# Layer two's first expert tile picked and turned on chip instead of read back from memory

## The chip, the cores and the metric

The kernel runs on one core of a Trainium2 chip. The metric is the device time of one launch in microseconds. The median of three runs is given where two kernels are compared; traces come from one profiled execution each.

## The reference, cut to what matters

Two layers over 520 tokens (512 of a prompt, 8 samples) of width 1024. Each layer is a token mixer, a normalisation, and a mixture of 16 experts with top 2 routing. The part around the change is the second layer's expert stage:

```python
x = layer_norm(ALPHA * x + mix, ln1_g, ln1_b)        # the normed rows, X in the kernel
combine = route(t, w_router, router_bias)            # (tokens, 16), two weights a token
h = jax.nn.silu(jnp.einsum('td,edf->tef', t, w_gate)) * jnp.einsum('td,edf->tef', t, w_up)
y = jnp.einsum('tef,efd->td', h * combine[:, :, None], w_down)
x = layer_norm(ALPHA * x + y, ln2_g, ln2_b)
```

The gate and up products are 1024 to 512, the down product 512 to 1024, all in float32.

## The kernel before, in words

**Tokens in tiles.** X holds the 520 rows as five tiles of 128 partitions (`NT` = 5; the last has 8 rows), 1024 columns each.

**Slots.** The router gives each token two experts. VectorE works out a slot for each of them: expert e has the slots 96 e to 96 e + 95 (`CAP` = 96), and what is over goes to tiles behind. `r_slot[token, 16 i + e]` holds slot + 1 if token tile i's row goes to expert e, else 0. `choose`, `count` and `place_rows` do this; `place_rows` ends with two index lists, after which `shares` (weights), `tables` (which expert each tile takes, how many tiles; semaphore `tab_set`) and eight diagonal matrices follow on VectorE.

**Scatter and rows back.** GpSimd writes every row of X to its two slots in the DRAM buffer `expert_rows`: ten indirect transfers (`scatter`, semaphore `scat`). ScalarE waits for all ten (`scat` at 320), then issues `load_rows` for tile 0 and tile 1 (four transfers each), and scales the five tiles of X by ALPHA in place. VectorE turns the loaded rows in 32x32 blocks (`turn_rows`), which gives `xeT`, the tile with the width on the partitions.

**A tile on TensorE.** An expert tile is 64 products for each of gate, up and down (two records each, 128 records a block), with the output of the tile before turned back behind the first quarter of gate (eight transposes). ScalarE applies silu to gate (`sg_set`); VectorE turns the *next* tile's rows once that is done, and then multiplies by up (`h_set`), which down waits for. Tiles run in pairs in a loop; this input fills 16 tiles in a layer.

**Weights.** Two sets of buffers, 2 MB each for gate, up and down. SyncE's queue loads the set of tile t + 2 as tile t frees each buffer: gate when tile t's gate product is done (`gate_ps`), up after its up product, down after its down product. The weights of experts 0 and 1 of layer two are loaded earlier, during the mixer.

**Fillers.** Between the counts and the loop of layer two TensorE runs `keep_clock(24, 2, 512)`: products of constants, whose results nobody reads.

**End.** After the loop the results are gathered from DRAM, weighed on TensorE and normed.

Of the kernel before, what the change touches and what calls it, by code (L numbers as in the profile page):

```python
# [20 lines left out]
PAGE, NPAGES, NPHYS = 128, 8, 80  # L21
PAST = PAGE * NPAGES
BATCHES = DB // 2
LATE = P + 64
E, GROUPS, EPG, F = 16, 4, 4, 512
KF = F // P
CTX = 15
# [21 lines left out]
def rows_of(i):  # L49
    return P if i < NT - 1 else DB  # L50


def constants():

    parts, place, at = [], {}, 0

    def put(name, a, *dims):
        nonlocal at
        full = np.zeros((P, int(np.prod(a.shape[1:]))), np.float32)
        full[:a.shape[0]] = a.reshape(a.shape[0], -1)  # L60
        parts.append(full)
        place[name] = (at, dims or a.shape[1:])
        at += full.shape[1]

    def rowwise(v):
        return np.broadcast_to(np.asarray(v, np.float32).reshape(1, -1), (P, np.size(v)))

    i = np.arange(P)
    put("ident", np.eye(P))
    put("ones", np.ones((P, P)))  # L70
    put("before", (i[:, None] < i[None, :]))

    half = ROPE // 2
    inv = (np.float32(10000.0) ** (np.float32(-2.0) * np.arange(half, dtype=np.float32) / np.float32(ROPE)))
    pos = np.concatenate([np.arange(SEQ), np.full(DB, PAST)]).astype(np.float32)
    ang = pos[:, None] * inv[None, :].astype(np.float32)
    cos, sin = np.cos(ang).astype(np.float32), np.sin(ang).astype(np.float32)
    rot = np.concatenate([cos.T, cos.T, -sin.T, sin.T])
    one = np.ones((NOPE, TOK))
    put("rope_q", -SCALE * np.stack([np.concatenate([one, rot]), np.concatenate([rot, one])], 1))  # L80
    def natural(t):
        out = np.zeros((P, NT, half), np.float32)
        for j in range(NT):
            out[:rows_of(j), j] = t[P * j:P * j + rows_of(j)]
        return out
    put("cos_k", natural(cos))
    put("sin_k", natural(sin))

    put("causal", np.concatenate([np.zeros((P, SEQ - P)), np.where(i[None, :] > i[:, None], BIG, 0.0)], 1))
    own = np.full((P, BATCHES, DB), BIG)  # L90
    for u in range(BATCHES):
        for ab in range(2):
            own[32 * ab:32 * ab + 32, u, 2 * u + ab] = 0.0
    put("own_sample", own)

    band = np.zeros((P, 2, 4, BAND), np.float32)
    band_s = np.zeros((DB * CTX, 4, DB), np.float32)
    own_s = np.zeros((DB, 4, DB), np.float32)
    for g, w in enumerate(WINDOWS):
        for c in range(BAND):  # L100
            for r in range(max(0, c - w + 1), min(P, c + 1)):
                band[r, 0, g, c] = 1.0 / min(c + 1, w)
                band[r, 1, g, c] = 1.0 / w
            if c < P:
                band[c, :, g, c] -= 1.0
        for b in range(DB):
            band_s[b * CTX + CTX - w + 1:(b + 1) * CTX, g, b] = 1.0 / w
            own_s[b, g, b] = 1.0 / w - 1.0
    put("band", band)
    put("band_s", band_s)  # L110
    put("own_s", own_s)

    e = np.arange(E)
    put("slot0", rowwise(e * CAP))
    put("slot_over", rowwise((E - 1) * CAP - e * CAP))
    put("steps", rowwise(CAP * np.arange(1, KOV + 1)))
    put("before_e", rowwise(e[None, :] < e[:, None]), E, E)
    j = np.arange(EPG)
    put("earlier", rowwise(j[None, :] < j[:, None]), EPG, EPG)
    put("prefer", rowwise(GROUPS - np.arange(GROUPS)))  # L120
    put("real_row", (i < DB).astype(np.float32)[:, None])
    put("no_row", (i >= DB).astype(np.float32)[:, None])
    put("over_k", rowwise(np.arange(NOV)))
    put("even_k", rowwise(np.arange(0, NOV, 2)))
    put("expert", rowwise(e))
    put("reserve", rowwise(np.where(e < DENSE, 0, DB)))
    put("routed", rowwise(e >= DENSE))
    put("dense_row", np.where(e[None, :] < DENSE, TILES * CAP + DB * e[None, :] + np.minimum(i, DB - 1)[:, None], 0))
    put("ln_eps", np.full((P, 1), LN_EPS))
    put("rms_eps", np.full((P, 1), RMS_EPS))  # L130

    put("fold4", (i[:, None] % 32 == i[None, :] % 32))
    put("fold2", (i[:, None] % 64 == np.arange(64)[None, :]))
    return np.concatenate(parts, 1).astype(np.float32), place


def build(nc, t, consts_shape, place):

    ctx = ExitStack()
    with ctx:  # L140
# [119 lines left out]
        yl = [(ya[i], yb[i]) for i in range(3)] + [(view(arena, at, D), view(arena, at + D, D)) for at in (2048, 0)]  # L260
        diag = view(arena, 13104, NT - 1, 2, P)
        sum_at = (0, 2, 6, 4)
        mid_diag = view(C, place["rope_q"][0] + 512, 2, 2, P)
        alpha_id = view(C, place["causal"][0], P)

# [6 lines left out]
        def rt(n, *dims):  # L272
# [87 lines left out]
            sem(n) for n in ("lg_zero", "lg_ps", "lg_exp", "sel_set", "cnt_ps", "idx_set", "tab_set",  # L360
                             "scat", "xscaled"))
        dense, dense_st = sem("dense"), sem("dense_st")
        gath = [sem(f"gath{s}") for s in range(3)]
        diag_set, sum_ps, last_gath3, last_gath4 = (sem(n) for n in ("diag_set", "sum_ps", "last_gath3", "last_gath4"))
        last_gath, last_rows = gath + [last_gath3, last_gath4], (96, 96, 64, 32, 32)
# [51 lines left out]
        def _(sp):  # L417
# [55 lines left out]
            sp.wait_ge(pv_ps, 1)  # L473
            load_pages(sp, 0, 0, page_ld[0])
            load_pages(sp, 0, 1, page_ld[0])
            sp.dma_start(view(arena, 14656, LATE), t["consts"][:, held:]).then_inc(fold_ld, 16)
            load_pages(sp, 1, 0, page_ld[1])
            load_pages(sp, 1, 1, page_ld[1])
            sp.wait_ge(zero_st, 16 * (PAIRS - 1))
# [20 lines left out]
            for L in range(2):  # L500
# [20 lines left out]
                else:  # L521
                    sp.wait_ge(S[0]["xeT_set"], 2 * nh + 1)
                    sp.wait_ge(S[0]["xe_ld"][1], 64 * (nh + 1))
                    sp.dma_start(pscale, bcast(t["pool_scale"][0])).then_inc(st_ld, 16)
                    sp.dma_start(state[0:DB * CTX, :], t["state_pool"][0].rearrange("b c d -> (b c) d")).then_inc(st_ld, 16)

                    for slot, rows in ((0, 64), (1, 64), (2, 32)):
# [34 lines left out]
        def _(pe):  # L562
# [344 lines left out]
            def pool(i):  # L907

                pe.wait_ge(ln_out[0], NT + i + 1)
                if i < 4:  # L910
                    for g in range(2):
                        b = turn()
                        for c in range(4):
                            k = 4 * g + c
                            out = bank(b, 4, P)[:, c, :]
                            for at in (0, 64):
                                last = nc.tensor.matmul(out[at:at + 64, :], X[:, i, P * k + at:P * k + at + 64],
                                                        band[:, min(i, 1), k // 2, 0:P], start=True, stop=(i == 0))
                            for at in (0, 64) if i else ():
                                last = nc.tensor.matmul(out[at:at + 64, 0:CTX], X[:, i - 1, P * k + at:P * k + at + 64],  # L920
                                                        band[:, 1, k // 2, P:BAND], start=False, stop=True)
                        last.then_inc(turn_ps, 1)
                else:
                    b = turn()
                    pe.wait_ge(st_ld, 32)
                    for k in range(KD):
                        out = bank(b, KD, DB)[:, k, :]
                        for at in (0, 64):
                            nc.tensor.matmul(out[at:at + 64, :], state[0:DB * CTX, P * k + at:P * k + at + 64],
                                             band_s[0:DB * CTX, k // 2, :], start=True, stop=False)  # L930
                        for at in (0, 64):
                            last = nc.tensor.matmul(out[at:at + 64, :], X[0:DB, 4, P * k + at:P * k + at + 64],
                                                    own_s[0:DB, k // 2, :], start=False, stop=True)
                    last.then_inc(turn_ps, 1)
# [186 lines left out]
                router(1, i)  # L1121
            keep_clock(9, 2, 256)
            counts(3, 0, NT)
            keep_clock(24, 2, 512)
            experts(1)
            pe.wait_ge(xscaled, 2 * NT)
            pe.wait_ge(diag_set, 2)
# [112 lines left out]
        def _(act):  # L1240
# [103 lines left out]
            def experts(L):  # L1344
# [13 lines left out]
                    act.sem_inc(q["y_st"][s], 16)  # L1358

                if L:  # L1360
                    act.wait_ge(scat, 320)
                    load_rows(act, L, 0, slice(0, CAP))
                    load_rows(act, L, 1, slice(CAP, 2 * CAP))
                    for i in range(NT):
                        scale_rows(i)
# [112 lines left out]
        def _(dve):  # L1478
# [400 lines left out]
            def tables(L):  # L1879
# [16 lines left out]
                link(v.tensor_reduce(r_nov[one, :], r_nh[one, 0:NOV // 2], AXX, ALU.add))  # L1896
                v.tensor_scalar(n_half[one, :], r_nov[one, :], float(E // 2), None, ALU.add).then_inc(tab_set, 1)

            def experts(L):
                q = S[L]  # L1900
                dve.wait_ge(tab_set, 2 * L + 2)
# [6 lines left out]
                                xe[s].rearrange("p a (i m) -> p a m i", i=32).bitcast(mybir.dt.uint32)  # L1908
                                ).then_inc(q["xeT_set"], 1)

                dve.wait_ge(q["xe_ld"][0], 64)
                turn_rows(0, CAP if L else WIDE)
                if L == 0:
                    choose(0, 2, NT - 1, NT)

                def rows_back(tl, s, count):
                    dve.wait_ge(q["back_ps"], tl + 2)
# [59 lines left out]
            v.memset(bank(6, NT * E), 0.0).then_inc(lg_zero, 1)  # L1977

            dve.wait_ge(wp_ld, 16)
            dve.wait_ge(st_ld, 32)  # L1980
            v.tensor_scalar(alpha_id, ident, ALPHA, None, ALU.mult)
            wp4 = wpool.rearrange("p (g k) d -> p g k d", g=4)
            v.tensor_tensor(wp4, wp4, pscale.rearrange("p (g d) -> p g d", g=4).unsqueeze(2).to_broadcast([P, 4, 2, 256]),
# [10 lines left out]
            choose(1, 3, 0, NT)  # L1994
            count(1, 3, 0, NT)
            place_rows(1, 3, 0, NT)
            shares(1)
            tables(1)
            dve.wait_ge(mix_ps, 2 * NT)
# [60 lines left out]
```

## Time and profile before

| what | value |
|---|---|
| median of 3 runs | 1109.82 us (1109.48 to 1110.19) |
| the profiled execution | 1110.86 us |
| its span | 1109.2 us |
| TensorE busy | 1039.2 us (94%) |
| VectorE busy | 377.2 us (34%) |
| ScalarE busy | 195.8 us (18%) |
| GpSimd busy | 94.9 us (9%) |
| mean granted TensorE clock | 0.975 |
| moved by DMA | 297.24 MB, mean 268 GB/s |

The span runs from the first to the last instruction; the profiled time also holds what lies around it. The granted clock is TensorE's share of full speed. PE is TensorE, DVE is VectorE, ACT is ScalarE, POOL is GpSimd, SP is SyncE; a q behind a name is that engine's queue of transfers. A line number L is a line of the kernel. "x" counts instructions; a float32 product shows as two records, a transpose as one.

### The profile page before, as it was taken

Reading aid. Unit: us, or ns where it says so; the run is one execution under the profiler, and the core shown is the slowest. Engines: PE = TensorE matmul, PEld = TensorE weight load, DVE = VectorE, ACT = ScalarE, POOL = GpSimd, SP = SyncE. Lnnn points to the kernel's source line nnn. Section 1 sums busy time; section 2 is a strip of 40 time slices with the busy share of each in tenths; the row PEclk is TensorE's granted clock in tenths of the full one; section 3 lists DMA queues with packets and bytes.
Section 4 is the critical chain, followed back from the end, with each engine's and each line's share of the span. In section 5 each row is a group of like instructions: output and inputs, shape, how many; then the busy total and the mean of one; then the engine's idle time right before and its main releaser. Section 6 shows DMA issues by size and latency. Waiting matters only on the chain.

```text
span 1109.2 us, 36492 instructions
## 1 busy us (share of the span) xinstructions
PE 1039.2 (94%) x16051; PEld 878.1 (79%) x16051; DVE 377.2 (34%) x858; ACT 195.8 (18%) x444; POOL 94.9 (9%) x179
## 2 busy tenths in 40 slices
PE   7989999989999798999999999998899999999995
PEld 6767777744566398999999997675699999999982
DVE  1334444423366532121221212976112212212127
ACT  1234444430043121000000001111200000100010
POOL 0011121241000200000000002101100000000012
PEclk9999999989999889999999999988899999999999
DMA  9512342714205899999999997861599999999935
GB/s 337 196 56 90 121 145 90 256 35 135 88 14 215 333 360 331 361 374 397 375 383 374 388 389 240 312 276 66 188 368 399 385 394 371 379 393 384 401 102 218
DMA packets 80479, 297.24 MB, mean 268 GB/s; under 512 B 10216, under 2 KB 40304, under 8 KB 72095
## 3 DMA queue, kind: packets, MB, share of 16 engines
q1 hardware_dynamic: 54327, 248.91, 60.6%
q10 hardware_dynamic: 17952, 25.24, 6.8%
q0 software_dynamic: 8144, 22.29, 5.7%
q8 instruction: 41, 0.67, 0.2%
q14 instruction: 15, 0.12, 0.0%
HBM read 255.91 MB, written 40.97 MB: 268 GB/s over the span
## 4 chain that ended last, share of the span: by engine, by line
PE 81%; DVE 8%; DMA 4%; issue 3%; POOL 2%; ACT 1%; SPq 0%; ACTq 0%; POOLq 0%; DVEq 0%
PE PS L1000 16%; PE PS L1023 16%; PE PS L1012 15%; PE PS L895 5%; PE PS L648 4%; PE PS L695 3%; PE PS L985 3%; PE PS L711 3%; PE PS L603 2%; PE PS L704 2%; PE PS L625 2%; POOL expert_rows L1178 1%; PE PS L668 1%; PE PS L798 1%; PE PS L685 1%
## 5 line engine op out<-in xcount | busy, mean ns | idle before, releaser
L1000 PE MATMUL PS<-arena,ring 128*64 128x96 f32 (+1 forms) x4096 | 186.7, 250 | 8.0 <-DVE arena L1907 8.0
L1000 PEld LDWEIGHTS PS<-arena,ring 128*64 128x64 f32 x4096 | 177.0, 139 | 14.7 <-issue 14.7
L1023 PE MATMUL PS<-arena,ring 128*64 128x96 f32 (+1 forms) x4096 | 178.3, 248 | 10.1 <-DVE arena L1943 5.4
L1023 PEld LDWEIGHTS PS<-arena,ring 128*64 128x64 f32 x4096 | 173.8, 138 | 12.0 <-DVE arena L1943 6.5
L1012 PE MATMUL PS<-arena,ring 128*64 128x96 f32 (+1 forms) x4096 | 175.8, 246 | 0.7 <-issue 0.6
L1012 PEld LDWEIGHTS PS<-arena,ring 128*64 128x64 f32 x4096 | 171.9, 137 | 1.1 <-issue 1.1
L1907 DVE STREAM_TRANSPOSE arena<-arena 128x768 uint32<-128x768 uint32 x34 | 54.3, 1597 | 138.2 <-ACT arena L1384 124.0
L1951 DVE COPY arena<-PS 128x384 f32<-128x384 f32 x32 | 17.8, 557 | 160.9 <-PE PS L1023 160.9
L1395 ACT ACTIVATE arena<-PS 128x384 f32<-128x384 f32 x32 | 15.7, 490 | 252.8 <-PE PS L1023 252.8
L895 PE MATMUL PS<-ring,arena 128*128 128x512 f32 x128 | 57.2, 607 | 0.7 <-issue 0.7
L576 PE MATMUL PS<-C 128*128 128x256 f32 (+1 forms) x160 | 52.2, 483 | 0.2 <-issue 0.2
L895 PEld LDWEIGHTS PS<-ring,arena 128*128 128x128 f32 x128 | 24.7, 195 | 31.2 <-issue 31.2
L576 PEld LDWEIGHTS PS<-C 128*128 128x128 f32 x160 | 31.0, 196 | 20.0 <-issue 17.5
L648 PE MATMUL PS<-arena,ring 128*128 128x260 f32 x192 | 44.9, 384 | 1.2 <-POOL ring L1146 0.8
L695 PE MATMUL PS<-ring 128*128 128x512 f32 (+3 forms) x128 | 40.7, 463 | 1.8 <-ACT ring L1279 1.2
L1371 ACT ACTIVATE arena<-PS 96x512 f32<-96x512 f32 x32 | 18.9, 592 | 127.8 <-PE PS L985 119.6
L1919 DVE COPY arena<-PS 96x512 f32<-96x512 f32 x32 | 22.0, 687 | 56.7 <-PE PS L985 56.7
L648 PEld LDWEIGHTS PS<-arena,ring 128*128 128x128 f32 x192 | 35.2, 190 | 6.1 <-POOL ring L1146 1.0
L1157 POOL DMA_DIRECT2D ring<-cache_krope x64 | 34.5, 539 | 58.4 <-issue 58.4
L1287 ACT ACTIVATE ring<-PS,small 128x512 f32<-128x512 f32 (+1 forms) x64 | 33.0, 526 | 28.4 <-DVE small L1563 28.4
L695 PEld LDWEIGHTS PS<-ring 128*128 128x128 f32 x128 | 24.0, 198 | 17.1 <-issue 11.2
L1940 DVE TENSOR_TENSOR arena<-arena,PS 128x288 f32<-128x288 f32 (+1 forms) x32 | 14.6, 456 | 66.6 <-PE PS L1012 66.6
(300 smaller groups left out, 1113.1 us busy)
## 6 DMA issues: line engine op xcount, KB each, us to landing
ring<-w_up SPq DMA_DIRECT2D x32, 2048.0 KB, 18.1
ring<-w_down SPq DMA_DIRECT2D x32, 2048.0 KB, 20.9
ring<-w_gate SPq DMA_DIRECT2D x32, 2048.0 KB, 17.7
expert_out<-arena ACTq DMA_DIRECT2D x32, 384.0 KB, 13.9
arena<-expert_rows ACTq DMA_DIRECT2D x128, 96.0 KB, 9.5
expert_rows<-ring SPq DMA_DIRECT2D x6, 1920.0 KB, 9.9
ring<-cache_ckv SPq DMA_DIRECT2D x56, 128.0 KB, 2.2
expert_out<-ring SPq DMA_DIRECT2D x1, 4608.0 KB, 25.3
```

The lines of the kernel that those rows point to most:

```text
L576: nc.tensor.matmul(bank(b, cols), ident, idle_rows[:, 0:cols], start=True, stop=True)
L648: last = nc.tensor.matmul(bank(b, HALF), wuq[:, m, P * parity:P * (parity + 1)], cq[:, m, HALF * hf:HALF * (hf + 1)], start=(m == 0), stop ...
L695: nc.tensor.matmul(score(i), qT[par][:, P * i:P * (i + 1)], kT[par][:, 0:P * (i + 1)], start=True, stop=True).then_inc(s_ps, 1)
L711: last = nc.tensor.matmul(bank(3, 4, VH, off=256 * par)[at:at + 64, i, :], probT[:, i % 2, P * k + at:P * k + at + 64], V[odd][:, k, VH * ...
L895: last = nc.tensor.matmul(bank(b0 + hf)[0:n, :], oT[:, k, P * i:P * i + n], wo[:, k, 512 * hf:512 * (hf + 1)], start=(k == 0), stop=(k == ...
L985: last = nc.tensor.transpose(bank(4 + m // 4, 4, P)[0:CAP, m % 4, :], yT[:, m, :], ident)
L1000: last = nc.tensor.matmul(bank(s, KF, n)[at:at + 64, f, :], wg[w][:, k, P * f + at:P * f + at + 64], x[:, k, :], start=(k == 0), stop=(k = ...
L1012: last = nc.tensor.matmul(out[at:at + 64, :], wu[w][:, k, P * f + at:P * f + at + 64], x[:, k, :], start=(k == 0), stop=(k == KD - 1))
L1023: last = nc.tensor.matmul(bank(4 + m // 4, 4, n)[at:at + 64, m % 4, :], wd[w][:, f, P * m + at:P * m + at + 64], hh[:, f, :], start=(f == ...
L1157: pool_e.dma_start(krp[:, bass.ds(half, 1), ROPE * n:ROPE * (n + 1)], t["cache_krope"][0, bass.ds(page, 1), :, :].rearrange("a p d -> p a ...
L1287: nc.scalar.activation(prob[:, i, 0:P * (i + 1)], score(i), ACT.Exp, scale=-1.0, bias=mneg[:, c:c + 1], accum_out=rsum[:, c:c + 1]).then_i ...
L1907: v.transpose(xeT[n][s][:, :, 0:CAP].rearrange("p m (a j) -> p a m j", j=32).bitcast(mybir.dt.uint32), xe[s].rearrange("p a (i m) -> p a m ...
```

## The change

Tile 0 of layer two's loop no longer comes from `expert_rows`. After the slots are known, VectorE makes five 0/1 matrices `picked` (token rows x 96 slots: 1 where the row's slot for expert 0 is that column's). TensorE multiplies them with X, 512 columns at a time, over the five token tiles: this gives the 96 rows of tile 0 in two PSUM banks. ScalarE copies the halves to SBUF (`first_rows`), TensorE turns them by eight transposes (each of every eighth column), VectorE copies these into `xeT`. ScalarE only increments the semaphore of tile 0's rows in place of four loads. The filler products shrink. The slot numbers are 96 new columns of the constants, loaded by SyncE ahead of the pooling state; the scatters stay as they are, since tile 1 and later still read their rows back.

```diff
-LATE = P + 64
+LATE = P + 64 + 96
...
+    put("slot_no", rowwise(1 + np.arange(CAP)))
...
+        slot_no = view(C, place["causal"][0] + P, CAP)
+        first_rows = view(arena, 5120, D)
+        picked = view(C, place["rope_q"][0], NT, CAP)
...
+        picked_set, first_ps = sem("picked_set"), sem("first_ps")
...
                     sp.dma_start(pscale, bcast(t["pool_scale"][0])).then_inc(st_ld, 16)
+                    sp.dma_start(slot_no, t["consts"][:, held:held + CAP]).then_inc(st_ld, 16)
...
             counts(3, 0, NT)
-            keep_clock(24, 2, 512)
+            keep_clock(12, 2, 256)
+            pe.wait_ge(picked_set, 1)
+            for hf in range(2):
+                for i in range(NT):
+                    n = rows_of(i)
+                    last = nc.tensor.matmul(bank(hf)[0:CAP, :], picked[0:n, i, :], X[0:n, i, 512 * hf:512 * (hf + 1)],
+                                            start=(i == 0), stop=(i == NT - 1))
+                last.then_inc(first_ps, 1)
+            pe.wait_ge(picked_set, 3)
+            for k in range(KD):
+                last = nc.tensor.transpose(bank(2 + k // 4, 4, CAP)[:, k % 4, :],
+                                           first_rows[0:CAP, :].rearrange("b (p k) -> b k p", k=KD)[:, k, :], ident[0:CAP, 0:CAP])
+                if k % 4 == 3:
+                    last.then_inc(first_ps, 1)
             experts(1)
...
                 if L:
+                    for hf in range(2):
+                        act.wait_ge(first_ps, hf + 1)
+                        nc.scalar.activation(first_rows[0:CAP, 512 * hf:512 * (hf + 1)], bank(hf)[0:CAP, :], ACT.Copy
+                                             ).then_inc(picked_set, 1)
                     act.wait_ge(scat, 320)
-                    load_rows(act, L, 0, slice(0, CAP))
+                    act.sem_inc(q["xe_ld"][0], 64)
                     load_rows(act, L, 1, slice(CAP, 2 * CAP))
...
+            def pick_rows():
+
+                for i in range(NT):
+                    n = rows_of(i)
+                    ins = v.tensor_scalar(picked[0:n, i, :], slot_no[0:n, :], r_slot[0:n, E * i:E * i + 1], None, ALU.is_equal)
+                ins.then_inc(picked_set, 1)
...
-                dve.wait_ge(q["xe_ld"][0], 64)
-                turn_rows(0, CAP if L else WIDE)
                 if L == 0:
+                    dve.wait_ge(q["xe_ld"][0], 64)
+                    turn_rows(0, WIDE)
                     choose(0, 2, NT - 1, NT)
+                else:
+                    for c in range(2):
+                        dve.wait_ge(first_ps, 3 + c)
+                        ins = v.tensor_copy(xeT[CAP][0][:, 4 * c:4 * c + 4, :], bank(2 + c, 4, CAP))
+                    ins.then_inc(q["xeT_set"], 1)
...
             place_rows(1, 3, 0, NT)
+            pick_rows()
             shares(1)
             tables(1)
```

## Rows read from the trace of the kernel before

**Rows 1.** Windows: stretch; busy us PE, PEld, DVE, ACT, POOL; clock, DMA share, GB/s.

```profile
790.30:791.00 0.70, 0.63 (x8) 0.64 (x10) 0.00 (x0) 0.70 (x2) 0.00 (x0) 0.50 0.00 0
799.00:816.00 17.00, 17.00 (x397) 16.70 (x394) 3.55 (x5) 1.57 (x4) 0.00 (x0) 1.00 0.94 318
799.00:1064.00 265.00, 261.45 (x6011) 256.07 (x6008) 55.63 (x78) 23.88 (x46) 0.00 (x0) 1.00 1.00 377
943.50:960.50 17.00, 17.00 (x398) 16.70 (x396) 3.56 (x5) 1.57 (x3) 0.00 (x0) 1.00 1.02 379
977.50:995.50 18.00, 17.25 (x399) 16.80 (x397) 3.56 (x5) 1.57 (x3) 0.00 (x0) 1.00 1.03 394
```

**Rows 2.** Timeline of the SyncE queue, layer two's loop: start us, us, what.

```profile
798.96 0.35 SPq L488 DMA_DIRECT2D ring<-w_gate  x1
...
1033.40 0.40 SPq L496 DMA_DIRECT2D ring<-w_down  x1
```

**Rows 3.** DMA issues from 798 and from 1021: KB, us to landing.

```profile
ring<-w_down SPq DMA_DIRECT2D x1, 2048.0 KB, 13.6
...
ring<-w_down SPq DMA_DIRECT2D x1, 2048.0 KB, 30.2
```

**Rows 4.** Chain of waits, router of layer two to tile 0: start us, us, what.

```profile
768.48 0.25 DVE arena L1870
...
782.03 2.83 DMA expert_rows<-X,ids
...
788.66 1.58 DVE arena L1907
...
790.37 2.83 PE PS L1000 x32
793.20 1.45 PE PS L985 x8
...
804.04 5.28 PE PS L1023 x128
```

**Rows 5.** Timeline of GpSimd, the scatters.

```profile
769.90 1.01 POOL L1178 DMA_INDIRECT expert_rows<-X,ids  x1 [46.86 <-DVE ids L1877]
...
775.07 1.71 POOL L1178 DMA_INDIRECT expert_rows<-X,ids  x1 [0.30 <-issue]
...
782.03 0.85 POOL L1178 DMA_INDIRECT expert_rows<-X,ids  x1 [0.30 <-issue]
```

**Rows 6.** Timeline of TensorE, the fillers before layer two's loop.

```profile
764.17 20.80 PE L576 MATMUL PS<-C 128*128 128x512 f32 x48
```

**Rows 7.** Timeline of TensorE, the end of layer one's loop.

```profile
679.52 1.08 PE L985 MATMUL PS<-C,arena 128*96 128x128 f32 x8 [0.65 <-DVE arena L1951]
680.43 3.66 PE L1080 MATMUL PS<-X,C 128*128 128x512 f32 x8
```

**Rows 8.** Timeline of VectorE, diagonals and tile 0.

```profile
775.01 0.26 DVE L2001 TENSOR_SCALAR arena<-C,small 128x128 f32<-128x128 f32 x1
...
776.38 0.27 DVE L2002 TENSOR_SCALAR arena<-C,small 128x128 f32<-128x128 f32 x1
...
802.83 0.45 DVE L1940 TENSOR_TENSOR arena<-arena,PS 128x288 f32<-128x288 f32 x1 [1.91 <-PE PS L1012]
...
809.36 0.56 DVE L1951 COPY arena<-PS 128x384 f32<-128x384 f32 x1 [5.03 <-PE PS L1023]
```

**Rows 9.** Timeline of ScalarE and its queue, tile 0.

```profile
784.88 3.72 ACTq L406 DMA_DIRECT2D arena<-expert_rows  x8
788.65 2.00 ACT L1420 ACTIVATE X<-X 128x1024 f32<-128x1024 f32 x2 [30.21 <-issue]
...
793.51 1.28 ACT L1384 ACT_TABLE_LOAD   x1
798.80 0.49 ACT L1384 ACTIVATE arena<-PS 128x384 f32<-128x384 f32 x1 [4.01 <-PE PS L1000]
...
811.68 0.59 ACT L1371 ACTIVATE arena<-PS 96x512 f32<-96x512 f32 x1 [3.81 <-PE PS L985]
```

More of the change, by code:

```diff
@@ L475, in _ @@
             load_pages(sp, 0, 1, page_ld[0])
-            sp.dma_start(view(arena, 14656, LATE), t["consts"][:, held:]).then_inc(fold_ld, 16)
+            sp.dma_start(view(arena, 14656, P + 64), t["consts"][:, held + CAP:]).then_inc(fold_ld, 16)
             load_pages(sp, 1, 0, page_ld[1])
@@ L924, in pool @@
                     b = turn()
-                    pe.wait_ge(st_ld, 32)
+                    pe.wait_ge(st_ld, 48)
                     for k in range(KD):
@@ L1979, in _ @@
             dve.wait_ge(wp_ld, 16)
-            dve.wait_ge(st_ld, 32)
+            dve.wait_ge(st_ld, 48)
             v.tensor_scalar(alpha_id, ident, ALPHA, None, ALU.mult)
```

## The prediction, made before the changed kernel was timed

> **What bounds the kernel now.** I read the views in this order: busy time by stretch, the chain of waits between layer two's router and its first expert tile, each engine's timeline there, and the weight loads' issue and landing.
>
> By stretch, two things bound the expert loop one after the other [rows 1]. A tile takes 17.00 us while TensorE never rests, and from about 977 us on 18 us with 0.7 us of rest, because weights come late. Over the whole loop (799 to 1064 us) the DMA engines' share is 1.00. The last down weights are issued at 1033.40 and land 30.2 us later, at 1063.6, when the first tile's landed in 13.6 us [rows 2, 3]. So the backlog grows through the loop, and the last tile waits for a stream that has run without a break since 798.96, where the first tile's gate product freed its buffer. What moves that start, and keeps the stream fed, moves the end.
>
> Before the loop the chain goes: slots known on VectorE (768.48 + 0.25 = 768.73), ten scatters on GpSimd (769.90 to 782.03), their landing (784.86), the rows read back, a 32x32 turn (788.66, 1.58 us), tile 0 on TensorE at 790.37 [rows 4, 5]. The reader is to see that nothing before 784.9 is TensorE's: it runs dummy products [rows 6]. And the pause after them dropped its clock: the granted clock is 0.50, so 1.2 of 2.4 GHz, when tile 0 starts [rows 1], its first 32 records take 2.83 us where a quarter of a 128-record block's 5.28 is 1.32, and eight transposes 1.45 where they take 1.08 elsewhere [rows 4, 7]. Tile 0 pays about 1.9 us for that.
>
> **The change, part by part.**
>
> *Picks (VectorE).* Five compares of 128x96 after the slots. The nearest row is the 128x128 multiply by a column: eight from 775.01 to 776.65, 0.20 us apart [rows 8]. Each costs at most that, and at least the 0.1 that 96 of 128 columns leave of half of it; I take 0.17, so 0.85 us in all (0.5 to 1.0), and the picks are ready near 770.5. Queued behind them are shares, tables and the diagonals: the tables end 0.85 later, near 776, and who waits for those (ScalarE, TensorE, SyncE, GpSimd) needs them only after 776.
>
> *The picks beside GpSimd.* One scatter took 1.71 us instead of 0.85 to 1.01: the one that ran beside the eight multiplies [rows 5, 8]. That is 0.76 us for eight of them, so 0.5 us for five; bounds 0 and 0.85 (all of it). The scatters then land near 785.35. The Trainium skill (SBUF — State Buffer, "Who interferes with whom") says that a tensor_scalar in a two-port mode shuts GpSimd out for its whole length; by that rule the cost is the full 0.85 and an estimate of the end 0.35 us later than in the sum below. The trace leans the same way, with a smaller number.
>
> *Row products (TensorE).* The fillers shrink from 24x512 to 12x256 columns. 48 records of 512 columns took 20.80 us, 0.433 each [rows 6]; 24 of half the width take 5.2, from 764.17 to 769.4. Then 1.1 us of rest for the picks, and 2x5 products of 512 columns, two records each: 20 x 0.433 = 8.7 us, 770.5 to 779.3. The eight-row tile costs as much as the others.
>
> *Copies, transposes, copies.* ScalarE copies each half, 96x512, 0.59 us [rows 9]; it is idle. The second ends near 780.0. Eight transposes: 1.08 us [rows 7], though mine read every eighth column; bounds 1.08 and 1.45. VectorE copies two 128x384 pieces, 0.56 each by the same shape [rows 8]; the first lies beside the second four transposes, so 780.0 + 1.1 + 0.7 with the steps between. Tile 0's input is ready at **781.9** instead of 790.24. TensorE reads the loop count just before; after the first layer's loop it did so behind eight transposes without a gap [rows 7], so I take nothing, bound 2 us.
>
> *Tile 0, first half.* TensorE never rests over 1.2 us, so I take full clock: gate 5.28 + 1.08 = 6.4 us, free at **788.3** instead of 798.96, which is 10.6 us earlier: 8.4 from the start, the rest from the clock. Up ends at 793.6 instead of 804.04.
>
> *Tile 0, second half: a new wait.* Its down product needs the gate's activation, and what stands ahead of that in ScalarE's queue moves by far less than tile 0 does. It waits for the scatters (785.35), issues four row loads instead of eight (3.72 us for eight, so 1.9: 787.2), scales five tiles of X (788.65 to 793.51, so 4.86: 792.1), loads a table (1.28: 793.4), activates (0.49: 793.9) [rows 9]. VectorE then turns tile 1's rows ahead of the multiply: 1.6 us, 795.5, and multiplies, 0.45 [rows 4, 8]: 796.0. Before, this queue was done at 794.8, ahead of the gate product at 798.8, and nobody waited for it; now TensorE waits 2.4 us. Down takes 5.28 and ends at **801.3** instead of 809.3 [rows 4]: **8.0 us earlier**. All tiles after run 8.0 earlier while TensorE bounds.
>
> *The cover this gives.* Even if TensorE's part costs 2 us more than I say (slow clock, slow transposes, a late loop), up still ends before 796, and tile 0's end doesn't move. The row loads of tile 1 land by about 788, before use.
>
> *The stream.* Gate and up loads start 10.6 and 10.5 us earlier, the down load 8.0. 2.4 us more lie between the up and down issues, in which the engines may run dry. In the stretch after 798.96 they moved 318 GB/s at a share of 0.94 [rows 1], 3.3 MB of the 4.2 of gate and up by the time down was issued, so at the loop's mean of 377 some 2.4 us of work was left, and little of the gap is idle. The stream's end thus moves by 8.0 (no lead kept) to 10.6 us (all kept). I take 9.0, between the two and nearer the lower, since part of the gap may still run empty. The four row loads less (96 KB each) lie before the stream and don't count. The new load of the slot numbers (48 KB) stands in SyncE's queue at the end of layer one's loop, where TensorE next runs fillers until the gathered rows land, so I take nothing, at most the 0.35 us of one issue [rows 2].
>
> **Sum.** 1110.86 (the profiled execution; span 1109.2) - 9.0 = 1101.9. That execution is 1.04 above the median of the runs, so on the median's scale **1100.8 us**.
>
> **The rivals.**
>
> *A, the forecast:* end 8.0 to 10.6 earlier, 1099.2 to 1101.8. For: the DMA share of 1.00 and the late weights; the ScalarE chain's length is from rows. Chance 0.70.
>
> *B, the clock falls in the new 2.4 us wait.* For: it fell in the pause of 5.4 us now. Against: before this wait TensorE works nearly without rest for 30 us. Price: the 1.9 us that tile 0 pays now, moved to the down product: tile 0 ends 6.1 earlier, the stream about 7: 1102.8. Chance 0.13.
>
> *C, a smaller gain:* ScalarE or VectorE later than I say (scatters delayed by 2 to 5 us by compares and diagonals moved onto them). 1103 to 1107. Chance 0.06. *C', more than 10.6,* a better packed stream, 1098: 0.03.
>
> *D, no change.* If the stream's start didn't count, because its rate is set otherwise and slack is somewhere behind: the end stays at 1063.6 for the last weights. Against it stands that the last tiles wait for exactly these. Within 0.2%: 0.03.
>
> *E, slower.* One mechanism: the scatters read X while TensorE streams X for 8.7 us and while VectorE's picks hold GpSimd. All of tile 0's second half hangs on the last scatter's landing, so the change loses once that comes over 8 us later than 784.9. The only price in the trace is the 0.76 us above; against it also, the scatters now run beside dummy products that read on-chip memory all the time. A delay of 11 us would give 1113. Chance 0.05.
>
> **How the numbers follow.** From no change a measurement here tells about 0.2%, 2.2 us. Faster: A, B, C and C', 0.92; same 0.03; slower 0.05. The range runs from C' (1098.3) past B (1102.8) into C, 1104.6: A, B and half of C, over 8 in 10; the likeliest alone is 1099.2 to 1101.8.
>
> **What would show it.** Row products 8.7 us long from about 770.5; tile 0 at 781 to 783; the granted clock 1.00 there; gate weights issued near 788.3; TensorE waiting about 2.4 us inside tile 0 for VectorE's multiply, behind ScalarE's activation at 793.4; down weights issued near 801.3; the last tiles still waiting, the last down weights landing 8 to 10.6 earlier than 1063.6. The prediction is wrong if tile 0 starts after 784, if the clock is 0.50 in its down product, if scatters land after 786, or if the DMA share falls under 0.9 for more than 2 us between 794 and 802.

## The result, and the profile after

The changed kernel takes 1096.58 us (median of 4 runs, 1093.99 to 1098.70); the kernel before took 1110.01 beside it (1109.48 to 1113.74). The ratio is 0.9892, with a 95% interval of 0.9864 to 0.9920: 12 us faster, 8.9 to 15.1. The forecast was 1100.8 with 1098.3 to 1104.6; the measured time lies 1.7 us below that range. The direction and the place were right, the forecast gain was too small.

The chain of waits of the changed kernel, from the picks to tile 0 (start us, us, what):

```profile
768.16 0.89 DVE C L1926 x5
...
769.09 9.34 PE PS L1135 x20
...
778.46 0.60 ACT arena L1382
...
779.10 0.70 PE PS L1140 x4
...
779.82 1.03 DVE arena L1948 x2
...
780.98 2.24 PE PS L1006 x32
783.23 1.87 PE PS L991 x8
...
794.49 5.31 PE PS L1029 x128
```

It answers to [rows 4], and the scatters, the 32x32 turn and the rows read back are gone from it. The slots are known at 767.27 in this trace (768.73 before), so all is counted from there. The last row ends at 799.80. From the slots to the end of tile 0's down product (taken at VectorE's copy behind it) are 32.57 us, where 40.64 were: **8.1 us less, with 8.0 forecast**.

How it got there differs from the forecast. Windows of the changed kernel, with the columns of [rows 1]:

```profile
762.70:768.00 5.30, 5.30 (x26) 4.44 (x25) 4.46 (x22) 0.00 (x0) 0.00 (x0) 1.00 0.00 0
769.10:778.40 9.30, 9.30 (x20) 2.92 (x20) 6.34 (x30) 0.59 (x1) 7.17 (x8) 1.00 0.84 333
778.40:781.00 2.60, 1.17 (x11) 0.99 (x10) 1.02 (x2) 0.59 (x1) 1.99 (x3) 1.00 0.96 375
781.00:783.00 2.00, 2.00 (x32) 1.93 (x32) 0.00 (x0) 0.00 (x0) 0.01 (x1) 0.66 0.45 100
783.00:784.00 1.00, 1.00 (x8) 0.82 (x5) 0.00 (x0) 0.00 (x0) 0.00 (x0) 0.50 0.06 16
786.00:789.00 3.00, 3.00 (x78) 3.00 (x76) 0.00 (x0) 3.00 (x4) 0.00 (x0) 1.00 0.71 189
935.80:952.80 17.00, 17.00 (x398) 16.70 (x396) 3.54 (x5) 1.58 (x3) 0.00 (x0) 1.00 1.02 379
1003.80:1021.40 17.60, 17.19 (x397) 16.73 (x395) 3.54 (x5) 1.58 (x3) 0.00 (x0) 1.00 1.02 394
```

Between 778.4 and 781.0 TensorE is busy for 1.17 of 2.60 us (it waits for ScalarE's copy and VectorE's copies), after 9.3 us without rest. As tile 0 begins the granted clock falls, and by 783 it is 0.50, 1.2 of 2.4 GHz. The longest rest ahead of that since 762.7 was 0.98 us, for the picks. Tile 0's first 32 records took 2.24 us and its eight transposes 1.87. The last two windows are a tile while TensorE bounds (17.00) and one of the last three (17.60, with 0.4 us of rest for late weights).

GpSimd's scatters in the changed kernel (answers to [rows 5]):

```profile
768.44 1.01 POOL L1197 DMA_INDIRECT expert_rows<-X,ids  x1 [47.24 <-DVE ids L1900]
...
774.84 1.32 POOL L1197 DMA_INDIRECT expert_rows<-X,ids  x1 [0.30 <-DVE ids L1920]
...
780.16 0.86 POOL L1197 DMA_INDIRECT expert_rows<-X,ids  x1 [0.30 <-issue]
```

The five picks (to 769.05) lie beside the first scatter, which took 1.01 us as before: nothing of the 0.5 us forecast. The scatter beside the eight diagonals took 1.32 us, where it took 1.71 before and its neighbours take 0.95.

ScalarE and its queue, and VectorE, in the changed kernel (answer to [rows 8, 9]):

```profile
783.23 2.36 ACTq L411 DMA_DIRECT2D arena<-expert_rows  x4
785.63 1.06 ACT L1443 ACTIVATE X<-X 128x1024 f32<-128x1024 f32 x1 [6.58 <-issue]
...
790.49 1.28 ACT L1407 ACT_TABLE_LOAD   x1
791.79 0.49 ACT L1407 ACTIVATE arena<-PS 128x384 f32<-128x384 f32 x1
```

```profile
792.31 1.60 DVE L1937 STREAM_TRANSPOSE arena<-arena 128x768 uint32<-128x768 uint32 x1 [11.46 <-ACT arena L1407]
793.83 0.41 DVE L1975 TENSOR_TENSOR arena<-arena,PS 128x288 f32<-128x288 f32 x1
```

The silu ends at 792.28, 25.0 us behind the slots (25.2 forecast), and VectorE's multiply at 794.24. But TensorE's up product ends only at 794.49, mostly because of the clock. So the 2.4 us wait forecast inside tile 0 isn't there: the two chains (TensorE's, and ScalarE's with VectorE behind it) end within 0.3 us of each other.

SyncE's queue and the landing of the first and the last down weights in layer two's loop, in the changed kernel (answer to [rows 2, 3]):

```profile
789.41 0.35 SPq L493 DMA_DIRECT2D ring<-w_gate  x1
...
799.84 0.38 SPq L501 DMA_DIRECT2D ring<-w_down  x1
...
1021.45 0.40 SPq L501 DMA_DIRECT2D ring<-w_down  x1
```

```profile
ring<-w_down SPq DMA_DIRECT2D x1, 2048.0 KB, 11.6
...
ring<-w_down SPq DMA_DIRECT2D x1, 2048.0 KB, 30.1
```

The gate weights are issued 22.1 us behind the slots, not 19.6, and so 8.1 us earlier than before, like the end of tile 0: the stream has no lead of its own. The backlog grows as before, and the last down weights land at 1051.6 instead of 1063.6, 12.0 us earlier. Of these 8.1 are the front, 1.5 stand already at the slots, and the rest arises in the loop behind tile 0 (257.4 instead of 259.9), where no instruction was changed. Counted from the slots, the last landing is 10.6 us earlier. Where the rest comes from is what most of the experiments are about.

### The profile page after: what moved, and what is told of

It reads as the page before. It is cut to its first block, busy times and chain, and to the rows that moved or that the text cites. A ratio compares the mean times of both kernels' runs of the same rounds, so it can differ in the third digit from the quotient of the medians.

```text
span 1097.0 us, 36506 instructions
## 1 busy us (share of the span) xinstructions
PE 1033.7 (94%) x16055; PEld 878.5 (80%) x16055; DVE 377.2 (34%) x864; ACT 197.1 (18%) x446; POOL 94.8 (9%) x179
## 4 chain that ended last, share of the span: by engine, by line
PE 83%; DVE 8%; DMA 4%; issue 2%; ACT 1%; POOL 1%; SPq 0%; POOLq 0%; DVEq 0%; ACTq 0%
PE PS L1006 16%; PE PS L1029 16%; PE PS L1018 16%; PE PS L901 5%; PE PS L654 4%; PE PS L991 3%; PE PS L701 3%; PE PS L717 3%; PE PS L609 2%; PE PS L710 2%; PE PS L631 2%; PE PS L674 1%; PE PS L804 1%; PE PS L691 1%; DMA arena<-expert_out,ids 1%
## 5 line engine op out<-in xcount | busy, mean ns | idle before, releaser
L582 PE MATMUL PS<-C 128*128 128x256 f32 (+1 forms) x136 | 38.1, 440 | 0.0
L991 PE MATMUL PS<-C,arena 128*96 128x128 f32 x264 | 36.5, 282 | 1.3 <-DVE arena L1986 1.3
L1407 ACT ACTIVATE arena<-PS 128x384 f32<-128x384 f32 (+1 forms) x32 | 15.8, 493 | 116.1 <-PE PS L1006 116.0
## 6 DMA issues: line engine op xcount, KB each, us to landing
ring<-w_gate SPq DMA_DIRECT2D x32, 2048.0 KB, 13.5
expert_out<-arena ACTq DMA_DIRECT2D x32, 384.0 KB, 11.3
```

Of the source, the lines that this page charges most:

```text
L582: nc.tensor.matmul(bank(b, cols), ident, idle_rows[:, 0:cols], start=True, stop=True)
L991: last = nc.tensor.transpose(bank(4 + m // 4, 4, P)[0:CAP, m % 4, :], yT[:, m, :], ident)
```

## The experiments

Times of one kernel spread by 4 to 17 us here (the kernel before: 1101.8 to 1116.4 over the 91 single runs of the experiments), so the ratios, each against the kernel before on the same chip, carry the verdicts, and a trace's sections carry the places.

**before_again, after_again, after_third.** No edit.

> The kernel before, unchanged, for a second trace of it. What is open: the changed kernel came out 13.4 us faster, of which its trace shows 8.1 between the router's slots and the end of tile 0, as worked out beforehand; some 4 us more went in layer one's expert loop and 2.5 in layer two's, where no instruction changed. Theory one (where the tensors lie in DRAM decides how fast the weight stream runs): both loops come out as long as in the first trace of before, 289.8 and 259.9 us, within 1 us. Theory two (the stream's speed varies from run to run): at least one of them differs from the first trace by 2 us or more. Time 1110, 1108.5 to 1111.5 by the first, 1105 to 1114 by the second.

> The changed kernel, unchanged, for a second trace. Theory one (placement in DRAM): layer one's loop 285.9 and layer two's from the end of tile 0 on 257.3, both within 1 us, time 1096 to 1097.5. Theory two (variation from run to run): they scatter by 2 us or more, and the median over more rounds moves towards 1110 less 8 to 9, so 1101 to 1102. Both: from the slots to the end of tile 0 32.5 us, within 0.3.

> The changed kernel once more, for more single times. Placement: 10 to 11 us under before. Chance: 8 to 9 us under before. From the slots to the end of tile 0 again 32.5 to 33.7 us.

Measured: before_again 1109.68 us, ratio 1.0018 (0.9993 to 1.0042); after_again 1097.82, 0.9892 (0.9856 to 0.9927); after_third 1095.05, 0.9878 (0.9853 to 0.9904). The second trace of before has 287.4 and 258.1 us for the loops against 289.9 and 259.9, so they do vary from run to run by 2 us. But by the ratios the changed kernel stays 12.0 to 13.5 us ahead over 12 more runs (one of them, at 1110.8, is left out of the ratio) and doesn't move towards 1101. That is more than chance alone was to give (8 to 9) and, in after_third, more than placement was (10 to 11). From the slots to the end of tile 0: 41.65 in before_again, 33.65 and 33.74 in the changed kernel, 1.0 to 1.2 us longer in each than in the first traces, because the half clock lasted longer: after_again's first 32 records take 2.83 us, and before_again's eight transposes 1.94. The front (from the slots to the end of tile 0) thus gained 8.0 us in the second pair as well.

Much of the spread of single times goes with the granted clock, too. The stretch up to layer one's first expert product holds no instruction that this change adds. Over the 16 traces it lasts 385.7 us with 14.3 us of it at the half clock (before_again), and 391.2 with 29.9 (narrow_again); the two quantities have a correlation of 0.98. What decides how long the clock stays low there no run shows.

**wide_only, wide_512.** The kernel before with unused columns in the DRAM constants; what the chip's own memory holds is the same.

```diff
-LATE = P + 64
+LATE = P + 64 + 96          # wide_512: + 512
...
+    put("slot_no", rowwise(1 + np.arange(CAP)))          # wide_512: "unused", 512 zeros
...
-            sp.dma_start(view(arena, 14656, LATE), t["consts"][:, held:]).then_inc(fold_ld, 16)
+            sp.dma_start(view(arena, 14656, P + 64), t["consts"][:, held + CAP:]).then_inc(fold_ld, 16)     # wide_512: held + 512
```

> The kernel before with the 96 constant columns added to the DRAM tensor and nothing else: no new load, no picks. It moves every tensor behind the constants by 49,152 bytes. Theory one (placement): faster than before by 4 to 6 us, 1104 to 1106, nearly all of it in the two expert loops. Theory two (run to run): equal to before within 1 us.

> The kernel before with 512 unused columns in the constants in DRAM (262,144 bytes), nothing else. Theory one of placement (where the tensors lie changes the weight stream): the median leaves that of before by 2 us or more, to either side. Theory two (the 2.1 us of the 96-column variant were chance): within 1 us of before.

Measured: 1105.84 us, 0.9979 (0.9957 to 1.0001), and 1107.18, 0.9982 (0.9955 to 1.0008). The intervals of both reach 1, so each alone is unclear. The 2.0 to 2.3 us lie between the two theories of wide_only: less than the 4 to 6 of the first, more than the 1 of the second. wide_512 just reaches the 2 us of its own first theory.

**narrow, narrow_again.** The changed kernel with the constants as narrow as before: the slot numbers are made on chip by one product and one addition, and their load is left out.

```diff
-                    sp.dma_start(slot_no, t["consts"][:, held:held + CAP]).then_inc(st_ld, 16)
...
             pe.wait_ge(S[0]["h_set"], 4 * nh)
+            nc.tensor.matmul(bank(6, CAP, off=320), ones, before[:, 0:CAP], start=True, stop=True).then_inc(first_ps, 1)
...
+            dve.wait_ge(first_ps, 1)
+            v.tensor_scalar(slot_no, bank(6, CAP, off=320), 1.0, None, ALU.add)
```

> The changed kernel with the constants as narrow as before: the slot numbers are made on chip, by one product of ones with the strictly upper matrix and one addition, so DRAM lies as in the kernel before. Theory one (placement): the front keeps its 8.1 us and the loops fall back to the lengths of before, 1101 to 1102. Theory two (run to run): the same time as the changed kernel within 1 us.

> The changed kernel with the constants in DRAM as narrow as before, once more, for more single times. Placement (96 more columns in DRAM are worth about 2 us): 2 to 3 us above the changed kernel of this call. Chance: within 1 us of it.

Measured: 1098.80 us, 0.9927 (0.9894 to 0.9961), and 1100.94, 0.9921 (0.9891 to 0.9952); the slots to the end of tile 0 take 32.54 us in both traces. With the constants as before, the change is worth 0.76% or 8.4 us, which is about what its front saves. narrow_again lies 5.9 us above after_third, which ran beside it on the same chip, where placement was to give 2 to 3.

**after_608, wide_load.** The changed kernel with 512 more unused columns; the kernel before with the 96 columns and their load.

```diff
 # wide_load, on top of wide_only
+                    sp.dma_start(slot_no, t["consts"][:, held:held + CAP]).then_inc(st_ld, 16)
```

> The changed kernel with 512 more unused columns in the constants in DRAM. In the seven traces of the changed kernel and its variants with 96 added columns TensorE loses at most 2.3 us to waits for nothing that the profile shows in layer one's first two expert tiles; in the seven others (before, its variants, the narrow ones) 2.7 to 4.6. If where things lie in DRAM decides this, the extra columns may undo it: 2.7 us or more of such waits and a time 2 to 3 us above the changed kernel. If it is the program of the change, it stays: at most 2.3, and a time 11 to 12 us under before. The front stays in both: 32.5 to 33.7 us from the slots to the end of tile 0.

> The kernel before with the 96 added columns and their load in SyncE's queue, but no picks: all that the change does ahead of layer two's router. If the 2 to 3 us lie in this part, such waits in layer one's first two tiles are at most 2.3 us, and the time is 2 to 3 us under before, at 1106. If they need the rest of the changed program: 2.7 us or more of them, and 1106 to 1109 as with the columns alone.

Measured: after_608 1098.71 us, 0.9893 (0.9864 to 0.9923); wide_load 1105.85, 0.9961 (0.9942 to 0.9980). So wider constants with their load, but no pick and no product, make the kernel before measurably faster, by 4.3 us (2.2 to 6.4), and more columns don't undo it.

The waits that these two were to tell by sit in layer one's first two tiles. TensorE's timeline there, rows with a wait for nothing that the profile shows: before, after, narrow, wide_load and after_608, in this order.

```profile
419.58 3.99 PE L1012 MATMUL PS<-arena,ring 128*64 128x104 f32 x85 [0.60 <-issue]
...
427.82 5.70 PE L1023 MATMUL PS<-arena,ring 128*64 128x104 f32 x85 [2.32 <-issue]
```

```profile
427.31 4.05 PE L1029 MATMUL PS<-arena,ring 128*64 128x104 f32 x85 [1.73 <-issue]
```

```profile
407.03 3.61 PE L1027 MATMUL PS<-arena,ring 128*64 128x104 f32 x76 [1.18 <-issue]
...
420.06 3.99 PE L1016 MATMUL PS<-arena,ring 128*64 128x104 f32 x85 [0.59 <-issue]
...
427.75 4.05 PE L1027 MATMUL PS<-arena,ring 128*64 128x104 f32 x85 [1.77 <-issue]
```

```profile
425.13 4.05 PE L1026 MATMUL PS<-arena,ring 128*64 128x104 f32 x85 [2.05 <-issue]
```

```profile
420.60 4.00 PE L1019 MATMUL PS<-arena,ring 128*64 128x104 f32 x85 [0.87 <-issue]
...
428.57 5.70 PE L1030 MATMUL PS<-arena,ring 128*64 128x104 f32 x85 [2.05 <-issue]
```

The reader is to see the last figure of each row: 2.92 us in sum before, 1.73 after, 3.54 in narrow, 2.05 in wide_load, 2.92 in after_608. The last is over the 2.7 us named, and its time stays at 0.9893. These waits are thus a part of the matter and not its measure.

The traces also tell what TensorE probably waits for there. The profile has a queue for instructions (q8, "instruction"), with transfers of 16 KB. One of these ends shortly before each of the nine waits above does: at 418.11 and 426.44 in the kernel before, where TensorE goes on at 419.58 and 427.82, and at 425.92 in the changed one, where it goes on at 427.31. In all nine it is 1.35 to 1.64 us. So these look like waits for code, in transfers that run beside the weights. No run tested it.

What does part the kernels is the sum of three sections of each trace, in which the weights stream: layer one's first two tiles, its other 14 with the stores, and layer two's 15 tiles behind tile 0 (from tile 0's first product in layer one to VectorE's last copy there, and from the copy behind tile 0 to the last copy in layer two):

| constants in DRAM | kernels | sum of the three sections, us |
|---|---|---|
| as before | before, before_again, narrow, narrow_again | 549.7, 545.6, 546.5, 548.2 |
| wider | wide_only, wide_512, wide_load | 545.5, 545.4, 543.8 |
| wider, with the change | after, after_again, after_third, after_608 | 543.3, 544.3, 544.6, 543.2 |
| wider, variants below | scale_later, fillers, both | 542.8, 543.4, 544.8 |

The means are 547.5 and 544.1: 3.4 us less with wider constants, 2.4 of them in layer one and 1.0 in layer two. The groups don't overlap, but they come within 0.1 us of each other (545.6 and 545.5), and the three sections were picked after the traces were seen. The other sections don't part that way.

The single times say the same without a choice of sections. I fitted two terms, one for wider constants and one for the picks, to 157 single times: before, before_again, wide_only, wide_512, wide_load, narrow, narrow_again, after_again (without the one at 1110.8), after_third and after_608. Each chip's own level was taken out. Wider constants give 3.2 us (2.1 to 4.2) and the picks 8.5 (7.2 to 9.8), and nothing beyond their sum shows (0.7 us more, -1.8 to 3.1). With the granted clock of each time taken out as well they are 3.0 and 7.8, so the clock is not what the width changes.

**light_before, light_after.** Half of each down weight left out of the loops' loads; the down product then reads old blocks for the other half, so the results are not the reference's.

```diff
-                sp.dma_start(wd[s], t["w_down"][L, bass.ds(e, 1), :, :].rearrange("a (k p) d -> p (a k) d", p=P)
+                sp.dma_start(wd[s][:, 0:2, :], t["w_down"][L, bass.ds(e, 1), 0:2 * P, :].rearrange("a (k p) d -> p (a k) d", p=P)
```

> The kernel before with half of the down weights left out of every load in the two expert loops (1 MB of 6 a tile; the product then reads two fresh and two old blocks, so layer values are others, in both kernels of this pair alike). Theory one (the stream of weights bounds the ends of the loops and brings the scatter of the times): no waits for weights, both loops at 17.0 us a tile from end to end, the rest of layer two's loop 15 x 17.0 + 3 = 255 to 256 us, single times within about 1 us of each other. Rival (something else scatters): the times still spread over 10 us.

> The changed kernel with the same loads halved. Theory one: without the stream's scatter the change shows as what its front saves: 8.1 us less than the halved kernel before, within 0.5. Rival (the change also speeds the loops up, by where the tensors lie or otherwise, through something other than the stream): 11 to 12 us less. If the stream's end follows its earlier start beyond tile 0's end (the 8.0 to 10.6 of the prediction), nothing of that can show here.

Measured: 1100.11 us (1096.82 to 1104.24), 0.9917 (0.9891 to 0.9944), and 1090.06 (1083.46 to 1093.52), 0.9818 (0.9789 to 0.9848). TensorE's waits for late weights are gone (180.00 us busy of 180 from 820 to 1000 in both), and by the ratios the kernel before is 9.2 us faster for it and the changed one 7 to 8 (0.9818 against 0.9878 to 0.9892). That much the stream's bound costs. But single times still spread over 7 and 10 us, so my theory that the stream brings the scatter fell. The difference, 10.1 us by the medians and 11.0 by the ratios, is nearer the rival's 11 to 12 than to 8.1, which suggests that the gain of the wider constants doesn't need a saturated stream. With six times each it doesn't show it. The two traces say in part why it is more than 8.1: the front takes 41.46 and 32.26 us, 9.2 less. In light_after the clock never fell:

```profile
773.48 1.54 PE L1006 MATMUL PS<-arena,ring 128*64 128x96 f32 x32 [0.75 <-DVE arena L1948]
786.48 5.50 PE L1029 MATMUL PS<-arena,ring 128*64 128x96 f32 x128 [1.06 <-DVE arena L1975]
```

The rests ahead of tile 0 are those of the changed kernel (0.68 and 0.75 us), with no filler in them, and still the first 32 records run at full clock. The wait that the prediction put inside tile 0 is there then, with 1.06 us.

**scale_later, fillers, both.** The two chains of tile 0.

```diff
 # scale_later, ScalarE
                     load_rows(act, L, 1, slice(CAP, 2 * CAP))
-                    for i in range(NT):
-                        scale_rows(i)
...
                         scale_rows(NT - 1)
+                    elif not more:
+                        for i in range(NT):
+                            scale_rows(i)
 # fillers, TensorE
+            keep_clock(2, 4, 256)
             pe.wait_ge(picked_set, 3)
...
+            keep_clock(2, 4, 256)
             experts(1)
```

> The changed kernel with ScalarE's five scalings of X moved behind the first silu of layer two, 4.9 us less ahead of it. Theory one (tile 0 is held by two chains of nearly the same length, the half clock on TensorE and ScalarE's queue): the silu comes with the gate product, tile 0 still ends 32.5 us after the slots, because TensorE runs its first products at a clock of 0.50; time as the changed kernel within 1 us. Rival (ScalarE's queue alone holds it): the end comes 2 us sooner.

> The changed kernel with two filler products (256 columns) behind the row products and two behind the eight transposes, where TensorE rests 0.7 us each. Theory one: the granted clock stays at 1.00 through tile 0, the first 32 records take 1.3 us instead of 2.2, and TensorE then waits 1.5 to 2 us for the silu chain, so tile 0 again ends 32.5 us after the slots, time as the changed kernel within 1 us. Rival (the clock alone holds it): 2 us sooner. Third (short rests aren't what dropped the clock): it falls to 0.50 all the same.

> Both edits at once. Theory one: 30.6 us from the slots to the end of tile 0, 1.9 less than the changed kernel, and the time 2 us under it. If the clock falls in spite of the fillers: 32.5 and no gain. In all three, layer one's loop (unchanged code) takes 285.5 to 290 us if its length is chance, and 285.5 to 286 if it belongs to the changed kernel's layout in DRAM.

Measured, from the slots to the end of tile 0: scale_later 32.59 us, fillers 32.09, both 31.16, beside 32.57 (33.7 where the half clock lasts longer). Times, in the same order: 1094.15 us, 0.9893 (0.9847 to 0.9938); 1101.05, 0.9930 (0.9900 to 0.9960); 1096.70, 0.9900 (0.9871 to 0.9929). TensorE and ScalarE in scale_later:

```profile
776.66 2.79 PE L1006 MATMUL PS<-arena,ring 128*64 128x96 f32 x32 [0.75 <-DVE arena L1949]
779.38 1.43 PE L991 MATMUL PS<-C,arena 128*96 128x128 f32 x8
...
790.03 5.45 PE L1029 MATMUL PS<-arena,ring 128*64 128x96 f32 x128
```

```profile
784.97 0.49 ACT L1405 ACTIVATE arena<-PS 128x384 f32<-128x384 f32 x1 [0.35 <-PE PS L1006]
785.36 4.83 ACT L1444 ACTIVATE X<-X 128x1024 f32<-128x1024 f32 x5
```

The silu now follows the gate product at once, and nothing is won: the first 32 records take 2.79 us, mostly at the half clock. In fillers:

```profile
775.29 1.54 PE L1006 MATMUL PS<-arena,ring 128*64 128x96 f32 x32
...
787.94 5.50 PE L1029 MATMUL PS<-arena,ring 128*64 128x96 f32 x128 [0.71 <-DVE arena L1977]
```

```profile
785.44 0.49 ACT L1409 ACTIVATE arena<-PS 128x384 f32<-128x384 f32 x1
```

The first 32 records take 1.54 us, at full clock, and 0.71 us of rest appear ahead of the down product, for VectorE behind the silu. By its ratio fillers is some 4 us slower than the changed kernel, where the same time was expected. Its trace shows a part: in the tile behind tile 0 TensorE loses 2.6 us to three waits of the kind above (0.22, 0.95 and 1.42 us), of which the changed kernel has none there.

The kernel with both edits:

```profile
779.82 1.54 PE L1006 MATMUL PS<-arena,ring 128*64 128x96 f32 x32
...
791.59 5.45 PE L1029 MATMUL PS<-arena,ring 128*64 128x96 f32 x128
```

Full clock and no rest. Each edit alone moves the bound to the other chain; together they win 1.4 us in the trace, where 1.9 were expected. That is too little for the times here to show: all three intervals overlap that of the changed kernel. As to time, no version was found that beats it clearly.

## Why the prediction was right and where it failed

**Right: the place and the size of the front.** 8.0 us forecast, 8.1 in the first pair of traces, and 8.4 by the times of the kernels with narrow constants. The tail of the kernel is unchanged (40.0 and 39.8 us behind the last copy), and what tile 0 gained arrives at the end.

**The term that failed: "The new load of the slot numbers ... I take nothing".** The load itself is hidden, as said. But its source makes the constants in DRAM wider, and the sum has no term for what that does elsewhere. It was worth 0.2 to 0.4%: the three ratios of before with wider constants are 0.9979, 0.9982 and 0.9961, on average 2.9 us. With 8.4 us for the front that is 11.3, where 11.9 to 13.5 were measured (ratios 0.9892, 0.9892, 0.9893 and 0.9878). The gain lies in the expert stages (3.4 us by the table above). What in them it shortens is open: the waits of layer one's first tiles go with it only in part, two widths do the same, and the order of the tensors in DRAM wasn't tried. That it works by where the tensors behind the constants lie is argued, not shown: no trace gives an address, and wider constants also change the rows that their own loads read.

**Two steps wrong that cancelled.** "TensorE never rests over 1.2 us, so I take full clock" failed: the clock fell to 0.50 after a stretch of 2.6 us with 1.17 busy. The row products took 9.3 us instead of 8.7. So gate was free 22.1 us behind the slots and not 19.6. For that, "now TensorE waits 2.4 us" failed as well. The paragraph on cover had this outcome: up to 2 us more on TensorE leave tile 0's end where it is. It was 2.35 us more at the end of the up product (27.2 us behind the slots instead of 24.9), about as much as the ScalarE chain covers. So the 8.1 us rest on that chain, whose length was forecast well, and it was luck that the clock cost no more: where it stayed low for longer, in after_again and after_third, tile 0 ended 1.1 to 1.2 us later. fillers and light_after show the wait as forecast in kind, at 0.7 and 1.1 us, once the clock holds; both shows how little is left when neither binds.

**The stream's lead, 8.0 to 10.6, taken as 9.0:** it needed the full clock, and was 8.1. The 0.9 us over 8.1 had a wrong reason and made the miss smaller: with 8.1 the sum would have given 1101.7. That the last weights still bind the end was right (30.1 us to land, waits in the last three tiles), and halving a part of the load took 9 us off the kernel before and 7 to 8 off the changed one.

**The picks beside GpSimd, 0.5 us:** nothing measured. The Trainium skill's rule (SBUF — State Buffer, "Who interferes with whom"), by which the cost would have been 0.85 us, isn't borne out by these five picks; the eight diagonals behind them did stretch a scatter, to 1.32 us.

**The rivals.** B (the clock falls in the new wait) didn't happen: the clock fell as tile 0 began, where the ScalarE chain covered it, and the short waits of fillers and light_after left it at 1.00. D was wrong, since the last landing moved with the stream's start. E was wrong too: the scatters let ScalarE load rows 16.0 us behind the slots against 16.1. C' (more than 10.6, by a better packed stream, chance 0.03) is nearest in number. But the stream moved 381 GB/s in the changed loop and 377 before, and layer two's loop behind tile 0 is shorter by 1.0 us on average with wider constants; most of what was missing lies in layer one. The spread was too narrow as well: 1110 as the start rested on three runs 0.7 us apart, when the kernel spreads over 14.6.

## What to carry to other kernels

When a chain is shortened, follow each engine to the next meeting point: here the down product needed ScalarE's queue, and that held the gain near 8 us whether TensorE's clock fell or not (tile 0 ended 32.1 to 33.7 us behind the slots). Don't take a new constant in DRAM for free because its load is hidden: build the kernel before with the same bytes added, and the changed one without them, and see whether the two effects add up. And take the spread from a dozen runs before a range is written: three close ones say little.

## What the runs showed of the hardware that was not expected

- 49,152 or 262,144 more bytes in the constants in DRAM went with a kernel of 1109 us being 0.2 to 0.4% faster (0.9979, 0.9982; 0.9961 with a load of the 96 columns). The cause is open.
- The granted clock fell to 0.50 after 2.6 us of which TensorE was busy for 1.17, its two rests 0.68 and 0.75 us long. It fell so in seven traces of the picks without fillers, and not in an eighth with the same rests (light_after: 1.00). With four small filler products in those rests it was at full speed in both traces (first 32 records 1.54 us instead of 2.17 to 2.83). So the rests alone don't decide it. The Trainium skill (TensorE: Matmul & The Clock Gate, "What's actually happening") says that activity releases a throttle that is the default; the kernel before agrees with that so far, with 0.50 behind a pause of 5.40 us and 1.00 from 799 on, in tile 0's up product [rows 1].
- Identical code up to layer one's experts spent 14.3 to 29.9 us at the half clock, and took 385.7 to 391.2 us with it.
- TensorE's waits for nothing that the profile shows, 0.22 to 2.32 us each, ended 1.3 to 1.6 us behind a 16 KB transfer on the queue of instructions in every case looked at (nine in layer one, three in fillers).
- Products of a 96-column one-hot operand took 9.33 us for 20 records of 512 columns, 0.467 each, where fillers took 0.433 [rows 6], both at a granted clock of 1.00. Why is open.
- Single times of an unchanged kernel on one core spread by 14.6 us of 1109, and a lighter weight stream didn't narrow that by much (7 and 10 us over six runs each).
